# Three joins of a two-block network: norm roots moved behind the products, first three weight parts side by side

## What is computed

```python
def rmsnorm(x, g):
    y = x * lax.rsqrt(jnp.mean(x * x, axis=-1, keepdims=True) + EPS)
    return y * g

# end of the first block
h = h + moe_out                          # 32 experts, rows added per token
x = rms_norm(h, norm_final_w)[:, N_META:]
# second block, l = 0
h = concatenate([meta_tokens_2, x])
h = h + 0.5 * rmsnorm(swiglu(rmsnorm(h, n[0]), ffn1_wi, ffn1_wo), n[1])
h = h + rmsnorm(hybrid_mixer(rmsnorm(h, n[2]), w_in, ...), n[3])
h = h + 0.5 * rmsnorm(swiglu(rmsnorm(h, n[4]), ffn2_wi, ffn2_wo), n[5])

def swiglu(x, wi, wo):                   # 1024 -> 2 x 2816 -> 1024
    a, b = jnp.split(x @ wi, 2, axis=-1)
    return (jax.nn.silu(a) * b) @ wo
# the mixer's first products: u_f, and b, c, h of the short convolution
#   b * conv3(c * h);  u_f goes through a Fourier transform;
#   16 columns of logits for the delta rule; later parts use rmsnorm(h, n[2]) again
```

## Time and profile before

| | before |
|---|---|
| median of 3 runs | 2846.05 us (2844.45 to 2851.13) |
| the profiled execution's own time | 2843.73 us |
| its span, from first to last instruction | 2842.3 us |
| TensorE matmul busy | 2655.5 us, 93% |
| TensorE weight load busy | 2041.9 us, 72% |
| VectorE busy | 1226.0 us, 43%, 2210 instructions |
| ScalarE busy | 881.9 us, 31%, 1311 instructions |
| GpSimd busy | 160.7 us, 6% |
| mean granted TensorE clock | 0.975 of full |

### The profile page before, as it was taken

The page is one execution under the profiler, slowest core; times in us unless marked ns, Lnnn a source line. Parts: engine busy times, 40 slices in busy tenths (PEclk is TensorE's granted clock), DMA queues, the critical chain, the costliest instruction groups (busy, mean ns, idle before and its releaser), DMA issues. The chain is left out here.

```text
span 2842.3 us, 37921 instructions
## 1 busy us (share of the span) xinstructions
PE 2655.5 (93%) x15928; PEld 2041.9 (72%) x15928; DVE 1226.0 (43%) x2210; ACT 881.9 (31%) x1311; POOL 160.7 (6%) x216
## 2 busy tenths in 40 slices
PE   8999999999699898999999989999999999799997
PEld 6778788677333333338999989878888785588886
DVE  4446566534433333344333345344545434533334
ACT  3334444432111111123322233244454422331222
POOL 0000000000100000000000000040412300000000
PEclk9999999999799999999999999999999999999998
DMA  3022111232899999982222212311111122223221
GB/s 138 16 69 67 56 60 56 62 112 72 318 382 391 396 397 395 402 338 89 82 90 90 87 55 80 107 56 45 61 56 57 56 74 105 75 96 96 97 89 59
DMA packets 78457, 385.78 MB, mean 136 GB/s; under 512 B 9176, under 2 KB 9432, under 8 KB 53072
## 3 DMA queue, kind: packets, MB, share of 16 engines
q1 hardware_dynamic: 71856, 357.14, 34.8%
q0 software_dynamic: 5712, 24.30, 2.5%
q10 hardware_dynamic: 720, 1.90, 0.2%
HBM read 372.67 MB, written 10.62 MB: 135 GB/s over the span
## 5 line engine op out<-in xcount | busy, mean ns | idle before, releaser
L204 PE MATMUL ps<-uTr,ringr 128*128 128x512 f32 (+1 forms) x1408 | 409.3, 336 | 0.0
L204 PE MATMUL ps<-muh,ringr 128*128 128x264 f32 (+1 forms) x1504 | 373.9, 340 | 13.3 <-DVE uTr L500 9.4
L204 PE MATMUL ps<-buh,ringr 128*128 128x512 f32 (+1 forms) x1312 | 348.1, 352 | 15.4 <-ACT hg L1089 9.5
L465 DVE TENSOR_TENSOR ringr<-ring,ringr 128x1024 fp32r<-128x1024 f32 (+1 forms) x215 | 258.6, 1211 | 163.0 <-ACT ringr L459 162.8
L204 PE MATMUL ps<-fuh,ringr 128*128 128x264 f32 (+1 forms) x1296 | 283.5, 324 | 13.2 <-DVE ful L500 13.2
L204 PEld LDWEIGHTS ps<-muh,ringr 128*128 128x128 f32 x1504 | 244.3, 192 | 41.1 <-issue 11.7
L204 PEld LDWEIGHTS ps<-uTr,ringr 128*128 128x128 f32 x1408 | 241.9, 191 | 23.0 <-issue 3.4
L204 PEld LDWEIGHTS ps<-buh,ringr 128*128 128x128 f32 x1312 | 219.5, 189 | 47.7 <-issue 15.6
L459 ACT CAST ringr<-ring 128x1024 fp32r<-128x1024 f32 (+1 forms) x215 | 219.6, 1036 | 106.9 <-DMA ring<-in_w_fi 36.7
L204 PEld LDWEIGHTS ps<-fuh,ringr 128*128 128x128 f32 x1296 | 204.2, 191 | 36.9 <-issue 10.0
L204 PE MATMUL ps<-rmore,exT 128*64 128x512 f32 x736 | 180.1, 616 | 27.9 <-DMA rmore<-in_w_ein 26.5
(11 more groups left out here) (448 smaller groups left out, 4321.1 us busy)
## 6 DMA issues: line engine op xcount, KB each, us to landing
rmore<-in_w_ein SPq DMA_DIRECT2D x92, 1024.0 KB, 29.3
rmore<-in_w_eout SPq DMA_DIRECT2D x48, 1024.0 KB, 29.0
ring<-in_w_ein SPq DMA_DIRECT2D x36, 1024.0 KB, 29.6
ring<-in_w_fi SPq DMA_DIRECT2D x54, 512.0 KB, 3.7
fmore<-in_w_fi SPq DMA_DIRECT2D x34, 512.0 KB, 3.8
ring<-in_w_hg SPq DMA_DIRECT2D x32, 512.0 KB, 3.8
ring<-in_w_eout SPq DMA_DIRECT2D x16, 1024.0 KB, 29.9
ring<-in_w_out SPq DMA_DIRECT2D x32, 512.0 KB, 3.8
```

What stands on the lines that cost most here:

```text
L204: return self.P.matmul(out, lhsT, rhs, start=start, stop=stop, skip_group_check=True)
L465: self.k.V.tensor_tensor(low, self.part(i), high.bitcast(F32), SUB).then_inc(self.rest.next(), 1)
```

## The change

A root is one number per token, so a product of un-rooted input times root equals the product of rooted input. The change uses that at the three joins:

- The input of the next stage is gain times `hT`, tile by tile, with no root: ScalarE makes its high part straight from `hT` (copy with a scale), VectorE its low part straight from `hT` (one operation). The 8 operations gain*root*`hT` before the products are gone.
- The first three parts' products run side by side in three PSUM pairs: for each tile, all three parts (`beside3`), then the next tile. The products wait for three parts' halves instead of one. The casts and rests of these three are placed in the stage before (`nxt.W.cast_act`, `rest_dve`), their loads too (`first_parts`, `ConvFourier.load`).
- The squares' sum comes after these products: ScalarE squares, VectorE gathers 8 tiles into one, TensorE makes 1 or 2 products with ones instead of 8 or 16 (`sum_pe` after `first_pe`; at join 2 after a fourth part), then Ln and Exp.
- The root is multiplied into the results. In a feed-forward stage VectorE multiplies the first part by the root (L2431), Silu reads that from SBUF, VectorE multiplies by the second part (L2436) and by the root again (L2438): two more operations for each of 44 pairs. In `ConvFourier` the Fourier part, the product c*h (by the root squared), the convolution's result and the logits' row get a multiplication each, and the rooted input, which later stages still use, is made beside the slices: two tiles in each, with high and low parts.
- At join 1 the 16 learned tokens go with their own gain and root as before; the other tokens' final norm is made beside the first group's pairs from the kept squares. The multiplications for the last expert tiles use banks 6 and 7.

```diff
+def beside3(k, banks, ws, xh, xl, r0, r1, t):
+
+
+    ins = []
+    for b, (wh, wl) in zip(banks, ws):
+        for p, (w, x) in enumerate(((wh, xh), (wh, xl), (wl, xh))):
+            for j, (c0, c1) in enumerate(split(r0, r1)):
+                i = k.mm(k.ps[:, b + j, 0:c1 - c0], w[t], x[t][:, c0:c1], t == 0 and p == 0, t == 7 and p == 2)
+        ins.append(i)
+    return ins
...
+class Entry:
...
+    def high_act(self, m, added):
+
+        k, c = self.k, slice(self.r0, L)
+        k.A.wait_ge(*added.at(m + 1))
+        k.A.activation(self.hi[:, m, c], k.hT[:, m, c], ACT.Copy, scale=self.gains[m]).then_inc(self.parts.high.next(), 1)
+
+    def low_dve(self, m):
+        k, c = self.k, slice(self.r0, L)
+        k.V.wait_ge(*self.parts.high.at(m + 1))
+        k.V.scalar_tensor_tensor(out=self.lo[:, m, c], in0=k.hT[:, m, c], scalar=self.gains[m],
+                                 in1=self.hi[:, m, c].bitcast(F32), op0=MUL, op1=SUB).then_inc(self.parts.low.next(), 1)
...
+    def first_pe(self):
...
+        banks = [self.bank[i] for i in range(3)]
+        for t in range(8):
+            norm.between_pe(t)
+            if t == 0:
+                ws = [self.W.halves_pe(i) for i in range(3)]
+            k.P.wait_ge(*norm.parts.low.at(t + 1))
+            ins = beside3(k, banks, ws, uh, ul, self.r0, L, t)
+        for i in range(3):
+            ins[i].then_inc(self.W.used.next(), 1)
+            self.give(banks[i], (self.mixed if i == 1 else self.rooted).at(i // 2 + 1))
+        norm.sum_pe()
...
-        W.cast_act(0)
         self.norm.root_act()
-        for m in range(8):
-            self.norm.high_act(self.pu, m)
-            if m in (3, 6):
-                W.cast_act(m // 3)
         for g in range(3):
             for j in range(self.NT[g]):
                 i, n = self.place(g, j), 8 * g + j
                 W.ahead_act(i, 3)
                 k.table(ACT.Silu)
-                if n >= 2:
-                    k.A.wait_ge(*self.ph.low.at(n - 1))
-                k.A.wait_ge(*W.used.at(i + 1))
-                k.A.activation(self.row(self.sg[:, n % 2, r0:L]), self.acc(self.bank[i]), ACT.Silu).then_inc(
-                    self.silu.next(), 1)
...
+                k.A.wait_ge(*self.rooted.at(n + 1))
+                s = self.sg[:, n % 2, r0:L]
+                k.A.activation(s, s, ACT.Silu).then_inc(self.silu.next(), 1)
...
                 W.ahead_dve(i)
                 s = self.sg[:, n % 2, r0:L]
+                V.wait_ge(*W.used.at(i + 1))
+                if n == 0:
+                    V.wait_ge(*self.norm.root.at(1))
+                V.tensor_tensor(self.row(s), self.acc(self.bank[i]), rb, MUL).then_inc(self.rooted.next(), 1)
...
+                V.tensor_tensor(self.row(s), self.acc(self.bank[i + 1]), self.row(s), MUL).then_inc(self.mixed.next(), 1)
+                V.wait_ge(*self.mixed.last())
+                V.tensor_tensor(self.row(s), self.row(s), rb, MUL).then_inc(self.prod.next(), 1)
...
         self.post.gather_dve(7)
+        if nxt:
+            nxt.W.rest_dve(1)
+            nxt.W.rest_dve(2)
         for m in range(8):
             self.post.scale_dve(y, self.gain1, y, m, self.y.at(17 + m))
-            if m:
-                self.add_dve(m - 1)
-        self.add_dve(7)
+            self.add_dve(m)
+            if nxt and m:
+                nxt.low_dve(m - 1)
...
             A.copy(two(self.ct[:, i]), k.wide(self.bank[j, 1])).then_inc(self.c_out.next(), 1)
+            if j == 0:
+                self.norm.root_act()
             W.ahead_act(part[2])
...
             if j == 0:
+                W.ahead_dve(part[0])
                 V.wait_ge(*self.zero.at(2))
+                V.wait_ge(*self.norm.root.at(1))
+                V.tensor_tensor(rb2, rb, rb, MUL).then_inc(self.rb_out.next(), 1)
...
+            V.tensor_tensor(self.uf[:, i, 0:L], self.uf[:, i, 0:L], rb, MUL).then_inc(self.f_root.next(), 1)
...
+            for m in (2 * j, 2 * j + 1):
+                V.scalar_tensor_tensor(out=k.uT[:, m, :], in0=k.hT[:, m, :], scalar=self.gains[m], in1=rb, op0=MUL,
+                                       op1=MUL).then_inc(self.scaled.next(), 1)
```

More of the change, by code:

```diff
@@ L2107, in dve, with act @@
-    def dve(self, exp):
-        for m in range(8):
-            exp.add_dve(4 * NE - 8 + m)
-            if m % 2:
-                self.gather_dve(m - 1)
-    def gather_dve(self, m):
-        k, V, sq, w = self.k, self.k.V, self.squares[m % 4], self.k.fin[:, 0, m:m + 1]
-        V.wait_ge(*self.square.at(m + 1))
-        if m:
-            V.wait_ge(*self.gathered.at(m // 2))
-            V.scalar_tensor_tensor(out=self.acc, in0=sq, scalar=w, in1=self.acc, op0=MUL, op1=ADD).then_inc(
-                self.gathered.next(), 1)
-        else:
-            V.tensor_scalar(self.acc, sq, w, None, MUL).then_inc(self.gathered.next(), 1)
+    def act(self, added, W):
+        k, A = self.k, self.k.A
+        k.table(ACT.Ln)
+        W.cast_act(0)
+        A.wait_ge(*self.small.at(6))
+        A.copy(k.uh[:, :, 0:NM], self.um).then_inc(self.mhigh.next(), 1)
+        for m in range(8):
+            A.wait_ge(*added.at(4 * NE - 7 + m))
+            A.activation(k.uh[:, m, NM:L], k.hT[:, m, NM:L], ACT.Copy, scale=k.fin[:, 1, m:m + 1]).then_inc(
+                self.parts.high.next(), 1)
+            if m in (1, 3):
+                W.cast_act(m // 2 + 1)
+            if m >= 3:
+                self.square_act(m - 3)
+        for m in range(5, 8):
+            self.square_act(m)
@@ new lines, in low_dve, with between_pe @@
+    def low_dve(self, m):
+        k = self.k
+        k.V.wait_ge(*self.parts.high.at(m + 1))
+        k.V.scalar_tensor_tensor(out=self.lo[:, m, NM:L], in0=k.hT[:, m, NM:L], scalar=k.fin[:, 1, m:m + 1],
+                                 in1=k.uh[:, m, NM:L].bitcast(F32), op0=MUL, op1=SUB).then_inc(self.parts.low.next(), 1)
+    def pe(self, exp):
+        self.exp = exp
+        for m in range(6):
+            exp.to_pe(4 * NE - 8 + m)
+    def between_pe(self, t):
+        if t == 0:
+            self.k.P.wait_ge(*self.mlow.at(1))
+        if t in (1, 2):
+            self.exp.to_pe(4 * NE - 3 + t)
@@ L2124, in root_act, with sum_pe @@
+    def sum_pe(self):
+        k = self.k
+        k.take(6)
+        k.P.wait_ge(*self.gathered.at(8))
+        k.mm(k.ps[:, 6, :], k.ones, self.acc, True, True).then_inc(self.sumsq.next(), 1)
+        k.give((6,), self.log.at(1))
     def root_act(self):
@@ L2164, in mean_pe @@
         self.bank = b = k.pair(4)
-        k.P.wait_ge(*self.rsum.at(8))
-        k.mm(k.ps[:, b, :], k.ones, k.sq[:, 0, 0:S], True, True).then_inc(self.mean.next(), 1)
+        k.P.wait_ge(*self.rsum.at(7))
+        k.mm(k.ps[:, b, :], k.ones, self.squares[:, 0, :], True, True).then_inc(self.mean.next(), 1)
         k.give((b, b + 1), self.rlog.at(1))
@@ L2451, in act1 @@
         k, A, y = self.k, self.k.A, self.tmp[:, 1]
-        A.wait_ge(*W.used.at(i + 1))
-        A.copy(two(self.bl), k.wide(self.bank["row"], 16)).then_inc(self.row_out.next(), 1)
         k.table(ACT.Sigmoid)
@@ new lines, in first_pe @@
+    def first_pe(self):
+        k, W, norm = self.k, self.W, self.norm
+        k.turn = 0
+        for x in (3, 0, 1):
+            self.bank[0, x] = k.pair()
+        banks = [self.bank[0, x] for x in (3, 0, 1)]
+        ws = [W.halves_pe(i) for i in range(3)]
+        for t in range(8):
+            k.P.wait_ge(*norm.parts.low.at(t + 1))
+            ins = beside3(k, banks, ws, tiles(norm.hi, 8), tiles(norm.lo, 8), 0, L, t)
+        for i, out in enumerate((self.f_out, self.b_out, self.c_out)):
+            ins[i].then_inc(W.used.next(), 1)
+            k.give((banks[i], banks[i] + 1), out.at(1))
@@ L3522, in __init__ @@
         self.pm, self.post = Parts(k, "mg"), Norm(k, NM, True)
-        self.sigs = [self.added, nxt.sumsq]
+        self.sigs = [self.added, nxt.parts.low, nxt.gathered, nxt.square]
         self.bank = {}
@@ L3671, in mixer @@
         end.pool()
-        k.join(*end.sigs)
-    k.sig.close(kept + nxt.sigs)
-    return [s.last() for s in end.sigs]
+    k.sig.close(kept + nxt.sigs + nxt.W.sigs)
+    return nxt, free
 def ktiles(w):
```

415 lines of the change are left out of this document (235 added, 180 removed).

## The result

| | before | after |
|---|---|---|
| median | 2846.77 us (2844.45 to 2851.13, 4 runs) | 2821.87 us (2815.71 to 2825.61, 4 runs) |
| ratio, 95% interval | | 0.9912 (0.9899 to 0.9925) |
| profiled execution, span | 2843.73, 2842.3 | 2822.4, 2820.7 |
| VectorE busy, instructions | 1226.0, 2210 | 1304.4, 2317 |
| TensorE matmul busy | 2655.5 | 2637.9 |

The changed kernel is 0.9% faster: 24.9 us by these medians, 21.3 by the profiled executions. Timed again in two later sets of rounds it had medians of 2823.57 and 2826.90, with ratios of 0.9927 (0.9911 to 0.9943) and 0.9936 (0.9919 to 0.9953), so about 21 us is the better figure. The forecast was 2830, with 2822 to 2840 as its range; the first median lies 0.13 us under that range, the two later ones inside it. More telling than the edge is that the forecast's sum had 15.3 us where the traces show 21.6.

A forecast was written before the change was run, and what follows sets the result against it. TensorE, at 93% of the span, was taken as the bound, idling at the joins. Gains of 1.4 + 3.3 + 10.6 = 15.3 us off 2843.73 gave 2828.4, a predicted median of 2830, range 2822 to 2840.

The forecast's parts named there:

- Work beside: Feed-forward pairs and group ends: 62 us of added VectorE multiplications cost nothing; in `ConvFourier`'s last slice 1.0 us lost.
- T: Moment the first three parts are done: 8.1, 17.0 and 17.3 us earlier at joins 1, 2 and 3.
- rival 4: At the joins each VectorE operation holds the engine longer, 1.2 us: 16 us slower, 2862; chance 0.05.
- What is given back at joins 1 and 3: Fourth part waits for root, cast and rest: a 3.9 us hole plus 1.75 for the clock; each join loses 6.7.
- Join 2: First three parts 17.0 us earlier, 12.7 lost again by holes near 3.0 and 5.2 us before the transposes.
- The price of the clock: At TensorE's holes: one of 2.3 us or more costs itself and 1.75 us of low clock behind it.
- The last slice's 1.0 us: In `ConvFourier`'s last slice nine more operations stand ahead of the four outputs: 1.0 us lost, between 0 and 5.
- rival 2: Deeper waits in `ConvFourier`'s slices: three lose 2 to 3 us each, 8 us gone, 2838; chance 0.14.
- Rival 3: Products at joins 2 and 3 do not start early, third part's load or rest 8 us late: 2846; chance 0.06.
- Rival 1: TensorE's clock stays up in the four new holes, saving 5 to 7 us: some 2825; chance 0.15.

The follow-up runs named there:

- e1: The kernel before, with `mean_pe` moved behind the third output part of FFN 1's group 0 and `late_act` to the fifth; 2838.19 us, ratio 0.9971.
- e2: The changed kernel with `mean_pe` put back right behind the eighth pair and `late_act` at the second output part; 2821.00 us, ratio 0.9911.

## Why the prediction was right or wrong

**The step that failed is a term that it put at nothing: `mean_pe` at the end of FFN 1's first group.** The paragraph "Work beside" costs the pairs and the groups' ends of the new kernel and never asks what TensorE waited for there in the old one. The diff moves `mean_pe` from behind the eighth pair to behind the third output part, moves `late_act` with it and drops `aside_act`. The old trace shows 4.29 us of idle at that product, released by L2158, with low clock behind it: more than the 3.73 us ahead of join 1's first part, to which the forecast gave a paragraph. e1 measured the term at 6.2 us; e2 shows that the kept squares alone take it away, too. With it the sum is 21.5 and the forecast 2824.5, against medians of 2821.87, 2823.57 and 2826.90.

That this comes within 0.1 us of the 21.6 in the traces is in part luck. Stretch by stretch, against the forecast, join 2 gave 2.6 more, join 3 2.1 less, join 1 0.4 less, the slices 0.5 more, and E came 0.4 later: these nearly cancel. (2828.4 and 2.3 make 2830.7 by the forecast's own sum, where it says 2830.)

**T, the end of the first three parts: right at joins 1 and 2, 1.0 us late at join 3.** Counted from the event that opens each stretch, join 1's came at 30.3 us (forecast 30.3), join 2's at 26.3 (26.4), join 3's at 26.6 (25.6). At join 3 the granted clock stood at 0.50 for 5.7 us from the first product (0.87 in the us from 2431, 1.00 from 2432), where the sum had 3.5; at joins 1 and 2 it did so for 3.3 and 3.0. VectorE's three operations for a tile take 2.10 us from scale to scale at join 2, TensorE was the bound as forecast:

```profile
1687.37 0.76 DVE L418 SCALAR_TENSOR_TENSOR uT<-uT,vec,rb 128x528 f32<-128x528 f32 x1
1688.16 0.71 DVE L2474 SCALAR_TENSOR_TENSOR hT<-uT,hT 128x528 f32<-128x528 f32 x1
1688.79 0.76 DVE L454 SCALAR_TENSOR_TENSOR cul<-hT,vec,cuh 128x528 fp32r<-128x528 f32 x1
1689.47 0.76 DVE L418 SCALAR_TENSOR_TENSOR uT<-uT,vec,rb 128x528 f32<-128x528 f32 x1
```

Starts lie 0.79, 0.63 and 0.68 us apart, each less than the row's own duration or about it, so rival 4 (1.2 us each, 2862) is out. It stood on a rule of the Trainium skill, "VectorE: DVE Perf Modes", section "The DRAIN you can't avoid"; these rows disagree with it again, as the earlier trace rows did. They fit another sentence of that section of the Trainium skill, which the forecast left out: a next operation that is not held starts earlier.

**What is given back at joins 1 and 3: right in kind, 0.8 and 0.4 us short.** The holes were forecast at 3.9 us and came at 3.63, released by the rest behind the root as named. But the fourth part then took 8.7 and 8.3 us in place of 5.88, 2.8 and 2.4 for the low clock, which lasted 6.0 and 5.6 us behind the hole, where the sum had 1.75 for 3.5. That and T make join 3's gain 8.5 in place of 10.6 (1.0 of T, 0.4 of the fourth part, 0.7 not traced) and join 1's 1.0 or less in place of 1.4.

**Join 2: gained 6.9 where 4.3 were forecast.** The fourth part came T + 2.15 (forecast T + 3.0) and kept the full clock, 5.9 us; the sum had it start later and pay 1.75. The forecast let ScalarE copy the Fourier part behind T. But side by side the three parts don't end together: in the last tile the Fourier part is done first, and its copy began 1.4 us before T (1706.61). The cast behind it was done by then, and the rest stood behind a memset on VectorE:

```profile
1705.19 0.60 ACT L2722 COPY cuf<-ps 128x528 f32<-128x528 f32 x1 [4.51 <-PE ps L207]
1706.61 0.94 DVE L2751 MEMSET cxb<- 128x1060 f32 x1 [0.17 <-issue]
1707.48 1.22 DVE L527 TENSOR_TENSOR ringr<-ring,ringr 128x1024 fp32r<-128x1024 f32 x1
```

These 2.6 us passed down the chain of sum, root, rest: transposes at T + 22.8 in place of T + 25.2. The holes at the logits' part (forecast 5.2, came 4.84) and ahead of the transposes (0.88) were right.

**The price of the clock.** "A hole of 2.3 us or more costs itself and 1.75 us" was taken from two holes, and one was misread. The forecast puts the low clock from 1693.36 on down to the 4.46 us of idle before it; in that trace the granted clock is already 0.50 over 1689 to 1693, so the engine had been at the low level since the product behind the hole of 2.32. Where the rule was used it was too cheap, by 0.6 to 1.1 us at the holes of 3.63 and by 0.3 at 4.84; the hole of 2.15 lies under its bound and says nothing against it.

**The last slice's 1.0 us, and rival 2.** Nothing: from TR to the Fourier products before their outputs is 77.5 us after (1806.92 less 1729.40) and 77.8 before (1820.84 less 1743.01), and the one wait behind them is 3.90 in both. Rival 3 (no early start) fell with the starts at 1281, 1688 and 2426. Rival 1 (the clock stays up) came true at one hole of four, and there because the hole was shorter than the forecast had it. Rival 2 (waits inside the later slices) fell: between the transposes and 1806.92 no wait of TensorE is shown.

## What to carry to other kernels

List every instruction that a diff moves, a single product included, and ask for each what its engine waited for in the old trace. The largest gain missed here was at a product of 1 us, whose wait of 4.3 us held the eight output parts behind it. When a dependency is taken off the front of a stage, whatever stood in the streams behind it (casts, rests, a sum) must be sorted again by what it really needs: some 20 us more lay in a few such moves, as much as in the change itself. Side by side pays where the tiles come slower than one part uses them (joins 2 and 3: 2.1 us a tile against 0.73), and costs where it makes the first product wait for the third part's weights (join 1).
